# Two chained transformer blocks on one core: GpSimd makes one weight rest per boundary, third tiles split early, roots on row quarters, a moved chunk, an end by halves

## What is computed

```python
def first_block(x, ...):
    h = x
    for layer in range(2):
        xn = _rms_norm(h, norm_g[layer, 0])
        m = _even_mixer(xn, ...) if layer % 2 == 0 else _sgu_mixer(xn, ...)   # linear + sparse attention; spatial gating
        h = h + _rms_norm(m, norm_g[layer, 1])
        f = jax.nn.relu(_rms_norm(h, norm_g[layer, 2]) @ w1[layer])
        h = h + _rms_norm((f * f) @ w2[layer], norm_g[layer, 3])
    return h

def second_block(x, c, ...):
    mod = jax.nn.silu(c) @ w_ada + b_ada                  # six rows of 1024
    sh1, sc1, g1, sh2, sc2, g2 = jnp.split(mod, 6)
    h = rms_norm(x, norm_mix) * (1.0 + sc1) + sh1
    x = x + g1 * token_mixer(h, ...)                      # dilated and forgetting attention, gated, then w_out
    h = rms_norm(x, norm_ffn) * (1.0 + sc2) + sh2
    x = x + g2 * swiglu(h, w_ffn_in, w_ffn_out)
    return rms_norm(x, norm_final)
```

## Time and profile before

| | |
|---|---|
| median of 3 runs | 2063.04 us (2062.58 to 2064.1) |
| the profiled execution | 2063.17 us; its span 2061.4 us |
| TensorE busy | 2031.8 us, 99% |
| VectorE / ScalarE busy | 1004.0 us, 49% / 702.5 us, 34% |
| GpSimd busy | 349.1 us, 17% |
| mean granted TensorE clock | 0.997 |
| weights read | 205.70 MB from HBM |

### The profile page before, as it was taken

The page is one execution under the profiler, slowest core; times in us unless marked ns, Lnnn a source line. Parts: engine busy times, 40 slices in busy tenths (PEclk is TensorE's granted clock), DMA queues, the critical chain, the costliest instruction groups (busy, mean ns, idle before and its releaser), DMA issues. The chain is left out here.

```text
span 2061.4 us, 27644 instructions
## 1 busy us (share of the span) xinstructions
PE 2031.8 (99%) x11274; PEld 1698.6 (82%) x11274; DVE 1004.0 (49%) x1388; ACT 702.5 (34%) x1013; POOL 349.1 (17%) x207
## 2 busy tenths in 40 slices
PE   9999999999999999999999999999999999999998
PEld 7876678888888999888888888788888788888886
DVE  5446748627344534725745425642543564332345
ACT  5355644222123422324322212443433243122222
POOL 2000005867820001000387000000000200000000
PEclk9999999999999999999999999999999999999999
DMA  7221023545533233223354232222222132332321
GB/s 221 72 60 42 22 92 124 180 135 167 172 111 113 62 98 97 76 88 113 125 181 153 82 103 98 87 83 72 83 62 76 68 102 83 112 102 83 101 102 62
DMA packets 138986, 209.46 MB, mean 102 GB/s; under 512 B 5306, under 2 KB 114040, under 8 KB 138872
## 3 DMA queue, kind: packets, MB, share of 16 engines
q1 hardware_dynamic: 129904, 180.89, 27.2%
q0 software_dynamic: 6912, 25.17, 3.7%
q10 hardware_dynamic: 2056, 1.76, 0.3%
HBM read 205.70 MB, written 2.10 MB: 101 GB/s over the span
## 5 line engine op out<-in xcount | busy, mean ns | idle before, releaser
L1310 DVE TENSOR_TENSOR w_lo<-w_raw,w_hi 128x2048 fp32r<-128x2048 f32 x151 | 350.3, 2320 | 567.0 <-ACT w_hi L694 566.9
L1979 PE MATMUL ps<-x_hi,w_hi 128*128 128x512 f32 x1248 | 494.4, 396 | 2.6 <-DVE w_lo L1310 1.8
L1981 PE MATMUL ps<-x_hi,w_lo 128*128 128x512 f32 x1248 | 486.4, 390 | 0.0
L1980 PE MATMUL ps<-x_lo,w_hi 128*128 128x512 f32 x1248 | 486.2, 390 | 0.0
L694 ACT ACTIVATE w_hi<-w_raw 128x2048 fp32r<-128x2048 f32 x152 | 290.7, 1913 | 507.7 <-PE ps L1981 401.6
L1979 PEld LDWEIGHTS ps<-x_hi,w_hi 128*128 128x128 f32 x1248 | 234.7, 188 | 59.3 <-issue 10.1
L1981 PEld LDWEIGHTS ps<-x_hi,w_lo 128*128 128x128 f32 x1248 | 234.3, 188 | 49.6
L1980 PEld LDWEIGHTS ps<-x_lo,w_hi 128*128 128x128 f32 x1248 | 234.5, 188 | 46.3 <-issue 0.5
L1979 PE MATMUL ps<-w_hi,h_hi 128*128 128x512 f32 x688 | 268.6, 390 | 1.3 <-DVE col_bias L1688 1.3
L1980 PE MATMUL ps<-w_lo,h_hi 128*128 128x512 f32 x688 | 268.5, 390 | 0.0
L1981 PE MATMUL ps<-w_hi,h_lo 128*128 128x512 f32 x688 | 268.3, 390 | 0.0
(11 more groups left out here) (367 smaller groups left out, 2729.4 us busy)
## 6 DMA issues: line engine op xcount, KB each, us to landing
w_raw<-in_ffn_w SPq DMA_DIRECT2D x64, 1024.0 KB, 5.4
ada_w<-in_w_ada POOLq DMA_DIRECT2D x48, 512.0 KB, 4.2
w_raw<-in_w_ffn_in SPq DMA_DIRECT2D x22, 1024.0 KB, 5.1
w_raw<-in_w_in SPq DMA_DIRECT2D x20, 1024.0 KB, 5.3
w_raw<-in_o_w_in SPq DMA_DIRECT2D x16, 1024.0 KB, 5.7
w_raw<-in_w_ffn_out SPq DMA_DIRECT2D x11, 1024.0 KB, 5.0
w_raw<-in_e_w_in SPq DMA_DIRECT2D x9, 1024.0 KB, 5.2
w_raw<-in_o_w_out SPq DMA_DIRECT2D x8, 1024.0 KB, 4.9
```

Source lines behind the costliest of these rows:

```text
L1310: nc.vector.tensor_tensor(w_lo[:, slot, :], w_raw[:, slot, :], w_hi[:, slot, :].bitcast(F32), ALU.subtract).then_inc(w_lo_ready, 1)
L1979: nc.tensor.matmul(dst, a_hi, b_hi, start=start, stop=False)
L1980: nc.tensor.matmul(dst, a_hi, b_lo, start=False, stop=False)
L1981: return nc.tensor.matmul(dst, a_lo, b_hi, start=False, stop=stop_)
```

## The change

1. **Head rests.** At all five boundaries the second head tile's rest, `head_split_lo(p, 1)`, is made by GpSimd (`head_rest`) rather than by VectorE. `normed(1)` stands ahead of `add_sum(2)` now. GpSimd does it between its other work: at 1 after `gla_ready`, at 2 after chunks 0 to 2, at 3 after the mixer's products, at 4 after chunk 5, at 5 after `mg_ready`.
2. **Third tiles.** In `post`, ScalarE and VectorE split the tile after the two head tiles at the end of it, and the splits in the next stage's first turns are left out.
3. **s_upb.** The rest of the tile `filler.by_pool + 2` is GpSimd's ("one at the third mixer's end").
4. **gn_spreads** takes 32 rows of the identity and of `gn_sum` instead of 128.
5. **Chunks.** 0 to 2 are built before boundary 2 and 3 to 5 in layer 1, and chunk 3 is taken in `f1_up1` behind its second tile, chunk 4 at the end of it.
6. **The end.** Token tile 3 is finished, squared, scaled and stored by halves of its columns.

```diff
+            def rest(n, src_hi, dst):
+
+                pool.wait_ge(w_hi_ready, n + 1)
+                pool.wait_ge(w_lo_ready, n)
+                nc.gpsimd.tensor_tensor(dst, w_raw[:, n % 2, :], src_hi.bitcast(F32), ALU.subtract).then_inc(w_lo_ready, 1)
+
+            def head_rest(p):
+
+                rest(S[HEADS[p]].first + 1, head_hi[p, 1][:, :], head_lo[p, 1][:, :])
...
-            for cc in range(4):
+            for cc in range(3):
                 ada_chunk(cc)
 
+            head_rest(2)
...
+            pool.wait_ge(mix_mm, 16)
+            pool.wait_ge(mix_evac, 16)
+            head_rest(3)
             pool.wait_ge(h2_ready, 2 + h2_base("f1_0") + 6)
-            ada_chunk(4)
-            ada_chunk(5)
-
+            for cc in range(3, 6):
+                ada_chunk(cc)
+
+            head_rest(4)
...
+            n = filler.by_pool + 2
+            rest(n, w_hi[:, n % 2, :], w_lo[:, n % 2, :])
...
+            pool.wait_ge(mg_ready, DK)
+            head_rest(5)
...
                 turned_hi(p, 1)
+                if p < 5:
+                    split_hi(n + 2, n % 2, loaded(n + 2), st.done + st.count + 1)
...
-            for t in range(NT):
+            for t in range(3):
                 act.wait_ge(h_ready, 20 + t + 1)
                 root_of(t, 40 + t, h[:, t, :], m[:, t, :])
+            first, second = slice(0, D // 2), slice(D // 2, D)
+            act.wait_ge(h_ready, 24)
+            chain.link(square_m(3, 43, h[:, 3, first], m[:, 3, first]))
+            chain.link(nc.scalar.activation(ss[:, 11:12], ss[:, 11:12], ACT.Identity, bias=small[:, 22:23]))
+            act.wait_ge(h_ready, 25)
+            chain.link(square_m(3, 44, h[:, 3, second], m[:, 3, second]))
+            nc.scalar.activation(root[:, 11:12], ss[:, 12:13], ACT.Sqrt, bias=ss[:, 11:12]).then_inc(squares, 1)
...
                 normed(0, e + 2)
+                normed(1, e + 3)
                 if partial:
                     add_sum(pass_no, 2)
-                normed(1, e + 3)
-                head_split_lo(p, 1)
                 turned_lo(p, 0)
...
                 turned_lo(p, 1)
+                dve.wait_ge(w_lo_ready, n + 2)
+                split_lo(n + 2, n % 2)
...
-                chunks = {(0, 1): {2: 0, 5: 1}, (0, 2): {2: 2, 4: 3}, (1, 1): {3: 4}, (1, 2): {2: 5}}
+                chunks = {(0, 1): {2: 0, 5: 1}, (0, 2): {2: 2}, (1, 1): {2: 3, 6: 4}, (1, 2): {2: 5}}
...
-                if filler.closes(j):
+                if filler.closes(j) and filler.tile(j) != filler.by_pool:
+                    dve.wait_ge(w_lo_ready, filler.tile(j) + 2)
                     split_lo(filler.tile(j) + 2, filler.tile(j) % 2)
...
                 normed(2 * a + 1, 36 + 2 * a + 1)
-                if a == 0:
-                    head_split_lo(5, 1)
                 turned_lo(5, a)
...
                 for hd in range(GLA_HEADS):
-                    nc.tensor.matmul(ps[:, 3 + hd, :], ident[:, 32 * hd:32 * hd + 1].broadcast_to([P, P]), gn_sum[:, :],
+                    r = slice(32 * hd, 32 * hd + 32)
+                    nc.tensor.matmul(ps[:, 3 + hd, :], ident[r, 32 * hd:32 * hd + 1].broadcast_to([32, P]), gn_sum[r, :],
                                      start=True, stop=True).then_inc(gn_spread, 1)
...
-                chunks = {(0, 1): {1: 0, 4: 1}, (0, 2): {1: 2, 3: 3}, (1, 1): {2: 4}, (1, 2): {1: 5}}
+                chunks = {(0, 1): {1: 0, 4: 1}, (0, 2): {1: 2}, (1, 1): {1: 3, 5: 4}, (1, 2): {1: 5}}
```

More of the change, by code:

```diff
@@ L438, in finished, with by_pool @@
                 return [j for j, k in self.during(phase) if k == self.depth(j) - 1]
+            @property
+            def by_pool(self):
+                return S["s_gate"].first + S["s_gate"].count - 1
             def tile(self, j):
@@ L574, in _ @@
             load_rows("g_down1", w_g2, 12)
-            for t in range(NT):
[L577 to L580, removed]
+            ends = [(t, slice(0, D)) for t in range(3)] + [(3, slice(0, D // 2)), (3, slice(D // 2, D))]
+            for i, (t, cols) in enumerate(ends):
+                sp.wait_ge(final_done, i + 1)
+                sp.dma_start(out[0].rearrange("(t p) d -> p t d", p=P)[:, t, cols], m[:, t, cols]).then_inc(stored, 16)
+            sp.wait_ge(stored, 16 * len(ends))
         @block.gpsimd
@@ L631, in _ @@
                 nc.gpsimd.tensor_tensor(o_gla[:, hd, :], o_gla[:, hd, :], e_t[:, 4 + hd, :], ALU.mult).then_inc(gla_value, 1)
+            pool.wait_ge(gla_ready, GLA_HEADS)
+            head_rest(1)
             ada_n = [0, 0]
@@ L1057, in turn @@
                 def turn(i, q, it):
-                    if part or i:
+                    if part or i > 1:
                         split_next(st, i, q, it)
@@ L1100, in _ @@
             for i in range(st.count):
-                if i:
-                    split_next(st, i, i, 0)
                 for f in range(2):
@@ L1140, in _ @@
             for i in range(6):
-                if i:
+                if i > 1:
                     split_next(st, i, 0, i // 2)
@@ L1707, in _ @@
             mlp_layer(0, 1, 12)
-            split_next(S["o_u0"], 1, 1)
             st = S["o_v"]
@@ L1764, in _ @@
             mlp_layer(1, 5, 28)
-            split_next(S["s_qk"], 1, 1)
+            dve.wait_ge(mm_done, S["s_qk"].done + 2)
             dve.wait_ge(f_made, 2)
@@ L1925, in _ @@
                 normed(2 * a + 1, 36 + 2 * a + 1)
-                if a == 0:
-                    head_split_lo(5, 1)
                 turned_lo(5, a)
+            dve.wait_ge(w_lo_ready, S["g_up0"].first + 2)
             def swiglu_pair(st, part, it, ahead):
@@ L1962, in _, with ended, scaled @@
             dve.wait_ge(rows_loaded, 16 * 5)
[L1963 to L1972, removed]
+            def ended(t, cols, done):
+                src = ps_flat[:, t * 1024 + cols.start:t * 1024 + cols.stop]
+                dve.wait_ge(mm_done, done)
+                chain.link(nc.vector.tensor_tensor(m[:, t, cols], src, g2_row[:, cols], ALU.mult))
+                nc.vector.tensor_tensor(h[:, t, cols], h[:, t, cols], m[:, t, cols], ALU.add).then_inc(h_ready, 1)
+            def scaled(t, cols):
+                c = (40 + t) % 16
+                nc.vector.scalar_tensor_tensor(m[:, t, cols], h[:, t, cols], rstd[:, c:c + 1], row_gain[:, cols],
+                                               ALU.mult, ALU.mult).then_inc(final_done, 1)
+            whole, halves = slice(0, D), (slice(0, D // 2), slice(D // 2, D))
+            for t in range(2):
+                ended(t, whole, sum_done(10, t))
+            for t in range(2):
+                rooted(40 + t)
+                scaled(t, whole)
+            ended(2, whole, sum_done(10, 2))
+            for half in range(2):
+                ended(3, halves[half], sum_done(10, 3) + half)
+            rooted(42)
+            scaled(2, whole)
+            rooted(43)
+            for half in range(2):
+                scaled(3, halves[half])
         @block.tensor
@@ L2124, in part @@
                     pe.wait_ge(w_lo_ready, st.first + i + 1)
+                    last = pass_no == 10 and (i, t) == (st.count - 1, NT - 1)
                     if ready is not None:
@@ L2134, in part @@
                                     i == 0 and kk == 0, i == st.count - 1 and kk == 1)
+                        if last and half == 0:
+                            o.then_inc(mm_done, 1)
                     return o
```

1 line of the change is left out of this document (removed).

## The result

The changed kernel took 2068.2 us in the median of 12 runs (2066.68 to 2074.0), the kernel before 2063.92 us beside it (12 runs). The ratio is 1.0022 with an interval of 1.0014 to 1.003: 4.3 us slower, just above the 0.2% (4.1 us) that such runs can tell. The prediction was 2065.4, range 2059.0 to 2069.5. One execution of all that follow, of b_upb, took 2696.99 us at a mean granted clock of 0.699 and is left out.

A forecast was written before the change was run, and what follows sets the result against it. TensorE was taken to bound the kernel, busy 2031.8 of 2061.4 us, with gains only in its short stops. The terms summed to +2.2 on the profiled 2063.17, giving 2065.4 us, range 2059.0 to 2069.5.

The forecast's parts named there:

- Bound, and where the gains lie: TensorE, busy 2031.8 of 2061.4 us, bounds the kernel; gains lie only in its short stops and slow work behind them.
- GpSimd's rest at boundaries 2 and 4: GpSimd's 4.57 us subtraction holds up VectorE's SBUF operations, so TensorE's head starts later: +3.4 and +4.1 us.
- The rival without cost: GpSimd's rests cost nothing at the boundaries, starting later or holding VectorE less: 2056.1 us, chance 0.17.
- Boundaries 1 and 3: GpSimd's rest beside joined(1), partly absorbed by free time on VectorE: +1.0 and +0.7 us, 0 to 3.7 each.
- the slower rival: The clock falls at boundaries 2 and 4, 1.6 us each: 2068.1, or 2069.2 with a longer f1_up1 stop; chance 0.27.
- the forecast's allowance of 0.5: Put in for the risk of clock falls after 3.0 us of idle at boundaries 2 and 4; 0 to +3.2.
- Chunk 4 at the end of f1_up1: TensorE waits there for ada_mod: a 3.0 us stop plus 1.6 for the clock, +4.6 us (2.9 to 5.7).
- gn_spreads, chunk 3, s_upb, third tiles, end: Gains: side-by-side row quarters -2.4, stop at f0_up2 -2.9, gate_t wait -4.5, weight-rest waits -1.2, -0.3, -0.3, halved last steps -0.6.
- The wait that the prediction puts at 335: A TensorE wait that the prediction listed among those that should be gone after the change.

The follow-up runs named there:

- b_upb: The kernel before with only the s_upb rest moved to GpSimd; 2058.82 us in the median of eleven, ratio 0.9977.
- a_dve24: The changed kernel with the second head tile's rest at boundaries 2 and 4 on VectorE again, in the order of before; 2060.11 us, ratio to before 0.9983.
- a_late24: The changed kernel with GpSimd's rests at boundaries 2 and 4 made to wait until normed(1) is done; 2062.59 us, ratio to before 1.0.
- a_quarters: The changed kernel with each of GpSimd's five head rests cut into four operations of 512 columns; 2064.45 us, ratio to before 1.0003.
- a_chunk4: The changed kernel with chunk 4 taken behind the fourth tile of f1_up1 instead of the sixth; 2059.46 us, ratio to before 0.998.
- a_order: The changed kernel with add_sum(2) ahead of normed(1) again at boundaries 2 and 4, GpSimd's rests kept; 2066.77 us, ratio to before 1.0017.
- b_chunks: The kernel before with only the chunk edits as in the changed kernel; 2066.83 us, ratio 1.0017.
- b_gn: The kernel before with only gn_spreads on row quarters; 2059.75 us, ratio 0.9977.
- b_third: The kernel before with only the third tiles' early split, the rests staying on VectorE; 2058.68 us, ratio 0.9979.

## Why the prediction came out as it did

- **Bound, and where the gains lie.** Right: but for gn_spreads' own 2.2 us and the start, the us gained or lost stand at stops of TensorE or in the clock behind one. The sign was forecast rightly (+2.4 against the median), yet the prediction gave "within 0.2%" 0.51 and "slower" 0.31, and +4.3 lies just in the second.
- **GpSimd's rest at boundaries 2 and 4.** The step that decided, and it held in mechanism and size: `joined(0)` ends 1.1 us behind GpSimd's subtraction, +3.5 and +4.0 for +3.4 and +4.1. a_dve24, a_late24 and a_quarters show the cause by taking the work away, moving it and cutting it. The rival without cost falls.
- **Boundaries 1 and 3.** At 3 +0.9 for +0.7. At 1 the table reads +1.9 for +1.0, but that is one execution. `joined(1)` was held for 1.74 us (3.02 for 1.28) in all five traces with the same rest there; the cost at the place, read in the same way, was 0.9 (a_dve24), 1.4 (a_chunk4), 1.5 (a_late24), 1.9 and 2.1 (a_order). The forecast lies at the low end.
- **The clock at 2 and 4.** It fell, as the slower rival said (0.55 in the window of 3.4 us above, and 0.50 from 1330.7 to 1334.1 at boundary 4), but it cost next to nothing here: the slowed transposes and products lie beside ScalarE's and VectorE's way to `x_lo`, which is as late. a_order shows that it is just behind: with `x_lo` earlier the slowed TensorE comes last at boundary 2. The rival had the event right and the price wrong, and the forecast's allowance of 0.5 was not needed. Its yardstick, the length of the stop, doesn't even sort the rows before: the clock fell behind 1.32 us at 629.93 and not behind 1.30 at 674.78.
- **Chunk 4 at the end of f1_up1.** This is the term that was mis-sized: 5.9 + 2.3 for 3.0 + 1.6, 3.6 us, more than the whole difference of 2.8 between forecast and median. The 3.0 is 1.3 and 1.7 for holds, less than one of the 2.4 us that I allowed each operation. Four operations were held, two of them on the unit before the last, where I hadn't looked: 1.9 + 2.0 + 0.7 = 4.6. Also, this chunk is taken by an operation with two SBUF operands, not by the copy of chunk 3; and the clock stayed low for longer than behind 629.93. a_chunk4 and b_chunks measured the term from both sides.
- **gn_spreads, chunk 3, s_upb, third tiles, end.** -2.2, -3.0, -4.6, -2.6 and -0.3 for -2.4, -2.9, -4.5, -1.8 and -0.6. The wait that the prediction puts at 335 is the one at 338.29. The end gained half: the two half scalings still follow the whole one of tile 2 on VectorE.
- **By chance.** The start was 1.2 us shorter in the profiled execution. It varies by as much between executions of kernels that have the same start, and it hid part of the miss in the spans. The other way, 0.9 of the 2.8 us between forecast and median is the kernel before, which ran at 2063.92 beside the changed one and not at the 2063.04 that the forecast starts from.

## What to carry to other kernels

Work that is moved to GpSimd costs VectorE up to its length (3.5 and 4.0 us of 4.6 here), if VectorE has SBUF operations on the path meanwhile, and cost nothing while VectorE read PSUM (a_late24 at boundary 2): give it the stretch, not only the engine. A use of GpSimd's or VectorE's result belongs in the middle of a stage, where TensorE has other tiles to go on with; two table entries were worth 8.7 us. A bundle of small edits is worth taking apart: of this one five pieces gain some 13 us together and two (the rests at four boundaries, chunk 4's place) lose 18, and without the two it is 13.2 us faster than before.

## What the runs showed of the hardware

- **The clock after one and the same stop.** The stop of 2.79 us for `gate_t`, with the same work before and behind it, was followed by a granted clock of 0.50 for 3.4 us in before and in b_gn (there from 1619.7 on), and of 1.00 in b_third and b_chunks. It isn't all chance of one execution, as the clocks of b_third's executions above show. What decides it, no run here shows. A fall is worth 1.6 us, and a part's worth that is read from times alone can be off by as much. B_upb's profile has a fall of its own, +1.6 us, behind boundary 4, where its code is that of before.
- **GpSimd's TENSOR_SCALAR holds VectorE only at its start.** In the rows of `f1_up1` above, VectorE's cast was held for 1.34 us and ended 1.4 us behind the start of the TENSOR_SCALAR of 1165.40. (It had begun 0.36 us ahead of that, while GpSimd issued a DMA.) The next two, with SBUF operands alone, took their 0.69 and 0.68 us at 1166.85 and 1167.45 while the TENSOR_SCALAR ran on until 1168.25. The Trainium skill, SBUF — State Buffer, SBUF: two separate sides, has the ports locked for the whole instruction; the traces show this for TENSOR_TENSOR (4.95 and 1.38 us above), and not for TENSOR_SCALAR.
- **The slowdown goes both ways.** The masks of `w_s` (eight selects on GpSimd) took 2.02 us in a_late24 beside VectorE's PSUM operations and 5.45 in the changed kernel beside its SBUF ones:

```profile
663.19 5.45 POOL L684 TENSOR_SCALAR_AFFINE_SELECT w_s<-w_s 128x128 f32<-128x128 f32 x8
```

```profile
670.18 2.02 POOL L685 TENSOR_SCALAR_AFFINE_SELECT w_s<-w_s 128x128 f32<-128x128 f32 x8
```

- **Four fp32 products of 32 rows each run side by side.** Their eight records start in two groups of four, at 156.37 and at 156.9, and take 1.14 us together, against 3.59 on 128 rows.
